# The last expanding block of each FFN in the merged form of all the others

## The reference

```python
def conv_ffn(h, w_up, conv_w, conv_b, w_down):
    S = h.shape[1]
    u = h @ w_up
    gate, val = u[..., :D_FF], u[..., D_FF:]
    gp = jnp.pad(gate, ((0, 0), (CONV_WIDTH - 1, 0), (0, 0)))
    conv = conv_b
    for i in range(CONV_WIDTH):
        conv = conv + conv_w[i] * gp[:, i:i + S]
    return (jax.nn.gelu(conv, approximate=True) * val) @ w_down

...
        f = conv_ffn(rmsnorm(x, norm_ffn_pre[layer]), ffn_w_up[layer], ffn_conv_w[layer],
                     ffn_conv_b[layer], ffn_w_down[layer])
        x = x + rmsnorm(f, norm_ffn_post[layer])
        if layer == N_A_LAYERS - 1:
            k_sh, v_sh = shared_kv(x, kv_norm, att_w_kv, pos)
```

## Time and profile before

| | |
|---|---|
| median of 3 runs | 1244.71 us (1244.69 to 1244.76) |
| the profiled execution's own time | 1244.93 us |
| its span, first to last instruction | 1243.1 us |
| granted TensorE clock, mean | 0.999 |
| busy: PE, PEld | 1231.4 us, 1109.2 us |
| busy: DVE, ACT, POOL | 806.7 us, 693.8 us, 143.6 us |

### The profile page before, as it was taken

One profiled execution on the slowest core, in us unless ns is written; L12 is line 12 of the kernel. 1 busy time (PEld: TensorE's weight loads), 2 busy tenths in 40 slices (PEclk: granted clock), 3 DMA queues, 4 the chain that ended last, 5 costly groups with the idle time before them and its releaser, 6 DMA issues.

```text
span 1243.1 us, 19259 instructions
## 1 busy us (share of the span) xinstructions
PE 1231.4 (99%) x7538; PEld 1109.2 (89%) x7538; DVE 806.7 (65%) x1225; ACT 693.8 (56%) x996; POOL 143.6 (12%) x178
## 2 busy tenths in 40 slices
PE   9999999999999999999999999999999999999997
PEld 8888888888888999999998888888999998999996
DVE  5566656767667566666666878677666666666554
ACT  6444335655555655555554766555676556566554
POOL 1000001200001000000000410430201500201500
PEclk9999999999999999999999999999999999999999
DMA  9544443755553543343443654545454352354331
GB/s 337 202 164 169 170 159 131 255 186 190 188 185 144 201 154 136 145 147 135 152 171 126 229 202 179 197 163 180 144 175 169 138 204 102 118 205 140 133 136 51
DMA packets 33847, 208.55 MB, mean 168 GB/s; under 512 B 3985, under 2 KB 4258, under 8 KB 16226
## 3 DMA queue, kind: packets, MB, share of 16 engines
q1 hardware_dynamic: 31986, 201.32, 45.6%
q0 software_dynamic: 1488, 5.78, 1.3%
q10 hardware_dynamic: 288, 0.27, 0.1%
HBM read 206.30 MB, written 1.05 MB: 167 GB/s over the span
## 4 chain that ended last, share of the span: by engine, by line
PE 93%; DVE 2%; ACT 2%; issue 1%; DMA 1%; POOL 0%; SPq 0%; DVEq 0%; POOLq 0%; ACTq 0%
PE pair L596 18%; PE pair L598 17%; PE pair L597 17%; PE pair L738 12%; PE pair L732 6%; PE bank L596 3%; PE bank L597 3%; PE bank L598 3%; PE bank L1033 1%; PE bank L1058 1%; PE bank L1041 1%; PE bank L851 1%; ACT whi L1460 1%; PE bank L1008 1%; PE bank L804 1%
## 5 line engine op out<-in xcount | busy, mean ns | idle before, releaser
L1979 DVE TENSOR_TENSOR wlo<-raw,whi 128x2048 fp32r<-128x2048 f32 (+5 forms) x208 | 431.9, 2081 | 214.6 <-ACT whi L1460 213.7
L1460 ACT ACTIVATE whi<-raw 128x2048 fp32r<-128x2048 f32 (+5 forms) x208 | 362.0, 1742 | 190.6 <-PE pair L598 164.3
L596 PE MATMUL pair<-whi,bhi 128*128 128x384 f32 (+3 forms) x528 | 189.3, 359 | 0.2 <-DVE blo L2625 0.2
L598 PE MATMUL pair<-whi,blo 128*128 128x384 f32 (+3 forms) x528 | 183.7, 348 | 0.0
L597 PE MATMUL pair<-wlo,bhi 128*128 128x384 f32 (+3 forms) x528 | 183.7, 348 | 0.0
L596 PE MATMUL pair<-whi,ahl 128*128 128x384 f32 (+3 forms) x416 | 153.5, 369 | 0.8 <-DVE wlo L1979 0.8
L738 PE MATMUL pair<-ahl,whi 128*128 128x512 f32 x640 | 153.2, 391 | 0.0
L597 PE MATMUL pair<-wlo,ahl 128*128 128x384 f32 (+3 forms) x416 | 149.1, 358 | 0.0
L598 PE MATMUL pair<-whi,ahl 128*128 128x384 f32 (+3 forms) x416 | 149.1, 358 | 0.0
L738 PEld LDWEIGHTS pair<-ahl,whi 128*128 128x128 f32 x640 | 117.5, 188 | 22.6
L596 PEld LDWEIGHTS pair<-whi,bhi 128*128 128x128 f32 x528 | 100.9, 191 | 9.6 <-DVE blo L2625 0.9
(11 more groups left out here) (322 smaller groups left out, 1886.4 us busy)
## 6 DMA issues: line engine op xcount, KB each, us to landing
raw<-wstream_d SPq DMA_DIRECT2D x136, 1024.0 KB, 4.9
raw<-wstream_d SPq DMA_DIRECT2D x56, 768.0 KB, 4.1
raw<-wstream_d SPq DMA_DIRECT2D x4, 832.0 KB, 4.3
raw<-wstream_d SPq DMA_DIRECT2D x4, 800.0 KB, 4.6
gain_row<-rows_d POOLq DMA_DIRECT2D x5, 512.0 KB, 4.0
arena<-mem_d POOLq DMA_DIRECT2D x2, 1024.0 KB, 6.7
raw<-wstream_d SPq DMA_DIRECT2D x4, 384.0 KB, 2.9
raw<-wstream_d SPq DMA_DIRECT2D x4, 288.0 KB, 2.7
```

The lines of the kernel that those rows point to most:

```text
L596: pe.matmul(out_ap, lhi, rhi, start=first, stop=False, skip_group_check=True)
L598: return pe.matmul(out_ap, llo, rhi, start=False, stop=last, skip_group_check=True)
L1460: act.activation(whi[:, n % RING, 0:width[n]], raw[:, n % RAW, 0:width[n]], ACT.Copy).then_inc(hi_ready, 1)
L1979: dve.tensor_tensor(wlo[:, n % RING, 0:width[n]], raw[:, n % RAW, 0:width[n]], whi[:, n % RING, 0:width[n]].bitcast(F32), ALU.subtract).th ...
```

## The change

Tile 21 of each FFN gets the merged form. PE does 16 matmuls of 256 columns and 16 of 512 for it instead of 48 of 256. ACT copies the right halves, DVE adds them into `f_u`, and the gate and value products read `f_u` instead of PSUM. The last value product now signals `gv_ready` (22 times a layer instead of 21, hence the changed counts on POOL and the changed wait on ACT), and the add signals `drained_v`.

```diff
--- before.py
+++ after.py
@@ -514,7 +514,7 @@
             def scale_gates(l, first, last):
 
                 for i in range(first, last):
-                    pool.wait_ge(gv_ready, l * (FF_TILES - 1) + i)
+                    pool.wait_ge(gv_ready, l * FF_TILES + i)
                     pool.tensor_tensor(f_gate[i % 2], f_u[i % 2][:, 0, :], rstd_row[:, :], ALU.mult).then_inc(gate_scaled, 1)
 
             def load_gain(row):
@@ -702,7 +702,7 @@
                             between.pop(0)()
                     w.chunk += 1
 
-            def up_tile(held=None, between=(), merged=True):
+            def up_tile(held=None, between=()):
 
                 p = begin_block("v")
                 between = list(between)
@@ -725,19 +725,15 @@
                     mm.then_inc(chunk_used, 1)
                     w.chunk += 1
                     return
-                if merged:
-                    for k in range(KD):
-                        for f in range(2):
-                            sl = slice((2 * k + f) * P, (2 * k + f + 1) * P)
-                            pe.matmul(pair[:, p, f, SEQ:2 * SEQ], wlo[:, slot, sl], ahi[:, k, :], start=k == 0, stop=False, skip_group_check=True)
+                for k in range(KD):
+                    for f in range(2):
+                        sl = slice((2 * k + f) * P, (2 * k + f + 1) * P)
+                        pe.matmul(pair[:, p, f, SEQ:2 * SEQ], wlo[:, slot, sl], ahi[:, k, :], start=k == 0, stop=False, skip_group_check=True)
                 for k in range(KD):
                     both = ahl[:, k, :, :].rearrange("p c s -> p (c s)")
                     for f in range(2):
                         sl = slice((2 * k + f) * P, (2 * k + f + 1) * P)
-                        if merged:
-                            mm = pe.matmul(pair[:, p, f, :], whi[:, slot, sl], both, start=False, stop=k == KD - 1, skip_group_check=True)
-                        else:
-                            mm = product(pair[:, p, f, 0:SEQ], whi[:, slot, sl], wlo[:, slot, sl], ahi[:, k, :], alo[:, k, :], k == 0, k == KD - 1)
+                        mm = pe.matmul(pair[:, p, f, :], whi[:, slot, sl], both, start=False, stop=k == KD - 1, skip_group_check=True)
                     if k == KD - 1:
                         mm.then_inc(chunk_used, 1)
                     if k % 2 and between:
@@ -982,7 +978,7 @@
                 for j in range(UPS + 1):
                     if j < UPS:
                         up_tile(held[0] if j == 0 else None)
-                        up_tile(between=() if j else [nothing, nothing, spread_rows], merged=j < UPS - 1)
+                        up_tile(between=() if j else [nothing, nothing, spread_rows])
                     if l and j == MEM_AT:
                         mem_turn(0, 0)
                     if j:
@@ -1625,10 +1621,9 @@
                     j = i // 2
                     passed()
                     p, n, _ = w.next_block("v")
-                    if i < FF_TILES - 1:
-                        act.activation(f_cross[i % 2], pair[:, p, :, SEQ:2 * SEQ], ACT.Copy).then_inc(cross_out, 1)
-                        if not (l and i == 2 * MEM_AT + 1):
-                            catch_up()
+                    act.activation(f_cross[i % 2], pair[:, p, :, SEQ:2 * SEQ], ACT.Copy).then_inc(cross_out, 1)
+                    if i < FF_TILES - 1 and not (l and i == 2 * MEM_AT + 1):
+                        catch_up()
                     if i == 0:
                         spread_row()
                     elif i < FF_TILES - 1:
@@ -1656,7 +1651,7 @@
                     if l and i == 2 * MEM_AT + 1:
                         catch_up()
                     if i == FF_TILES - 1:
-                        act.wait_ge(drained_v[p], n)
+                        act.wait_ge(gv_ready, w.up("gv"))
                         gv_high(i)
                     if i == FF_TILES - 1:
                         used(1)
@@ -2239,9 +2234,8 @@
                     cv, gl, gv, ug, uv = f_conv[i % 2], f_gelu[i % 2], f_gv[i % 2], f_u[i % 2][:, 0, :], f_u[i % 2][:, 1, :]
                     at = fc + i * 4
                     gate = f_gate[i % 2]
-                    if i < FF_TILES - 1:
-                        dve.wait_ge(cross_out, w.up("cross"))
-                        dve.tensor_tensor(f_u[i % 2], pair[:, p, :, 0:SEQ], f_cross[i % 2], ALU.add).then_inc(drained_v[p], 1)
+                    dve.wait_ge(cross_out, w.up("cross"))
+                    dve.tensor_tensor(f_u[i % 2], pair[:, p, :, 0:SEQ], f_cross[i % 2], ALU.add).then_inc(drained_v[p], 1)
                     if i:
                         dve.wait_ge(gelu_done, w.up("ff"))
                         dve.tensor_tensor(f_gv[(i - 1) % 2], f_gelu[(i - 1) % 2], f_u[(i - 1) % 2][:, 1, :], ALU.mult).then_inc(gv_ready, 1)
@@ -2252,8 +2246,8 @@
                     else:
                         if i == 0:
                             dve.wait_ge(spread_out, w.up("spread"))
-                            dve.wait_ge(drained_v[p], n)
-                        step(dve.tensor_tensor(gate, pair[:, p, 0, 0:SEQ] if i else ug, rstd_row[:, :], ALU.mult))
+                        dve.wait_ge(drained_v[p], n)
+                        step(dve.tensor_tensor(gate, ug, rstd_row[:, :], ALU.mult))
                         step(dve.tensor_scalar(cv, gate, cols[:, at + 2:at + 3], cols[:, at + 3:at + 4], ALU.mult, ALU.add))
                     step(dve.scalar_tensor_tensor(cv[:, 1:SEQ], gate[:, 0:SEQ - 1], cols[:, at + 1:at + 2], cv[:, 1:SEQ], ALU.mult, ALU.add))
                     dve.scalar_tensor_tensor(cv[:, 2:SEQ], gate[:, 0:SEQ - 2], cols[:, at:at + 1], cv[:, 2:SEQ], ALU.mult, ALU.add).then_inc(conv_done, 1)
@@ -2261,7 +2255,7 @@
                         gv_low(i - 1)
                     if i == FF_TILES - 1:
                         dve.wait_ge(gelu_done, w.up("ff"))
-                        dve.tensor_tensor(gv, gl, pair[:, p, 1, 0:SEQ], ALU.mult).then_inc(drained_v[p], 1)
+                        dve.tensor_tensor(gv, gl, uv, ALU.mult).then_inc(gv_ready, 1)
                     if l and i == 7:
                         rope_angles()
                         dve.wait_ge(mem_rstd_ready, 1)
```

## The result

| | before | changed |
|---|---|---|
| median time | 1244.58 us (1244.05 to 1245.05, 20 runs) | 1246.14 us (1245.42 to 1248.03, 20 runs) |
| the profiled execution's own time | 1244.93 us | 1246.16 us |
| its span | 1243.1 us | 1244.1 us |
| granted clock, mean | 0.999 | 0.998 |
| busy PE / DVE / ACT | 1231.4 / 806.7 / 693.8 us | 1232.1 / 807.6 / 693.7 us |

The ratio is 1.0015, with an interval of 1.0009 to 1.0022: the change costs 1.56 us. The predicted time was 1245.0 us, with a range of 1244.3 to 1245.9.

What follows compares the result with a forecast made beforehand. TensorE was taken to bound the kernel, busy 1231.4 of 1243.1 us. Layer 0's +0.45 and layer 1's -0.17 summed to +0.28 us on the median 1244.71, giving 1244.99, rounded to 1245.0 us; range 1244.3 to 1245.9.

Steps and rivals of the forecast that it cites:

- TensorE's gain: Tile 21's expanding block in both layers: merged form takes 5.57 us, a gain of 0.18 us a layer.
- The chain's delay: DVE at tile 21: the added copy and add make the gate product and the whole DVE chain 1.09 us later.
- the case at tile 3: Earlier copy right behind a gelu: gelu at 236.06, copy at 236.39, add on DVE at 237.07 us.
- The contraction of tile 21: First place: the weight load waits for the late low half; price 0.01 us at most in either layer.
- The second place, the new `x` of layer 0: Behind layer 0's FFN: TensorE waits for the second token tile's first quarter; layer 0 loses 0.45 us.
- Layer 1: Third place: the memory's key product comes before TensorE needs the new `x`; layer 1 gains 0.18 less 0.01 us.
- B: Chain's delay comes through in full, 1.1 us in layer 0, 0.9 in layer 1: 1246.7 us; it or part, chance 0.23.
- A: Only the TensorE gain shows; layer 0's wait for `x` is hidden by the 20 fillers: 1244.35 us, chance 0.10.
- D: The merged form saves more, or a buffer freed earlier sets something else free; no size given, chance 0.02.
- C: Longer TensorE pause near 397.2 us drops the clock to 1.2 GHz at layer 0's first key-value product: 1250.7 us, chance 0.03.

Runs made afterwards that it cites:

- the second: The changed kernel measured once more, unaltered, against the kernel before: 1245.88 us, ratio 1.0012.
- the merged form alone: Kernel before with TensorE's merged form at tile 21 in both layers, but cross sums neither copied nor added: 1244.98 us.
- the cut wait on the changed kernel: Changed kernel; in layer 0 transposes 0 to 3 wait only for the first half of the read sums, 4 to 7 for all: 1245.62 us.
- the changed one with the tiny instruction: Changed kernel plus a one-column VectorE copy in idle time behind layer 0's FFN: 1245.74 us.
- the last kernel: Kernel before with the merged form in layer 1 only, layer 0's wait at the bank cut in two, 12 and 1 fillers: 1244.57 us.
- the gate-first kernel: Changed kernel with copy and add at tile 21 halved, gate half added first, tile 20's value product ahead of the add: 1244.94 us.
- the one that has only the tiny instruction: Kernel before plus a one-column VectorE copy in idle time behind layer 0's FFN: 1244.98 us.

## Why the prediction was wrong

**TensorE's gain: right.** Tile 21 takes 5.56 us, 0.19 and 0.20 less. The isolated step of the Trainium skill (TensorE: Matmul & The Clock Gate, section Back-to-back issue gap) would, as an estimate, have given 0.04; the measured blocks decide.

**The chain's delay: right.** Predicted 1.09 us from the case at tile 3, measured 1.09: the copy directly behind the gelu, the add 0.68 later.

**The contraction of tile 21: nearly right.** The load waits 0.18 us on PEld in both layers, and the matmuls lose 0.04 us, where the step had 0.01 at most.

**The second place, the new `x` of layer 0: wrong, and this is the largest part.** The step said that TensorE waits for the first quarter of the second token half, that POOL's idle time swallows 0.3 us and the fillers another 0.35, and that 0.45 us are left. The update did slide by 0.74, as computed. But one instruction of DVE earlier, at the end of L2045's last pair, TensorE has another wait, `pe.wait_ge(post_ready, 2 + 4)`: the transposes write to the banks from which the sums are read. That wait ends ahead of POOL's idle time and ahead of the first token half's transposes, so it gets all of the delay, and its slack was 0.00 us: the load at 396.14 stood 0.05 behind 396.09. I took the 0.35 us in front of the second half's transposes for the slack of the boundary, without asking what started the first half's. The term is 1.09 us, not 0.45. The step also says that DVE has no pause up to L2045; it has one of 0.95 us before the first split, for ACT's rounding, in both kernels. That pause swallowed nothing, because ACT's rounding slid along, as the step says.

**Layer 1: right.** 0.17 predicted, 0.16 measured.

**Not foreseen.** With 1.09 in place of 0.45 and all else as it stood, the sum would have been 1244.71 + 1.09 - 0.17 = 1245.63 us, inside the range. The rest is what no step had. The 0.33 us at 701 us belong to the number of instructions on DVE and not to the change's work; 0.20 come back behind 885 us, 0.11 of them at 1025; and by the medians 0.2 to 0.3 us lie outside the span. With them: 1.09 + 0.33 - 0.16 - 0.20 + 0.3 = 1.4, near the 1.56 of the first comparison and the 1.25 of the second.

**The rivals.** B, the delay in full, was half right: in layer 0 in full, in layer 1 not at all. A and D didn't happen. C didn't either: the clock was 1.00 at a boundary with 1.35 us without a matmul, of which 1.13 in one pause, more than double the 0.5 us that I had weighed.

**What stays open.** The changed kernel, the merged form alone, the cut wait on the changed kernel, the changed one with the tiny instruction and the last kernel have a median of 2.02 to 2.1 us outside the span, all others 1.78 to 1.83. In these five it scatters: 17 of the 75 executions below 1.9 us, 27 above 2.5 and up to 3.73, where the others never exceed 2.04. No edit sorts them: the gate-first kernel has all of TensorE's change and 1.79. What happens in that time no trace here shows.

## What to carry to other kernels

Where an engine starts a stage directly behind a filler or just one hand-over (0.05 us here) after another engine's instruction, it may be waiting with a slack of zero even though no idle time is shown. Ask for each of its waits in order what released it, the first one first, and not only for the one with the freshest data: buffers to be freed are waits too. A merged form of a matmul moves work to other engines. At the last turn of a loop, this work heads the chain on which the next stage waits: in layer 0 it cost 1.09 us, and in layer 1, where TensorE had other work first, the same form gained 0.16. (What the form is worth in the middle of the loop was not measured here.) And where a change is worth less than 0.5 us, adding one idle instruction to the kernel before tells how much of a difference is only the place of the code.

## What was not expected of the hardware

One instruction on DVE starts 0.35 us later, or doesn't, and the traces sort by how many instructions its engine has had: the gap ahead of an add was 1.0 us in the eight traces with 0 or 2 instructions more than before and 1.4 us in the six with 1, and one column's copy 300 us earlier switches it. At 1025 us the gap ahead of L2620 sorts by this number too: 3.70 to 3.71 us in the three traces with no more instructions than before, 3.35 to 3.36 in the nine with one to three more, 3.18 to 3.19 in the two with four more. There the kernels with more work differ in other ways as well, save the one that has only the tiny instruction (3.36).

TensorE's pause of 1.1 us left the granted clock of the stretch at 1.00.
